# Dilated attention heads: the scaling of probabilities moves from VectorE to ScalarE

## The reference, cut to what matters

```python
DIL_GROUPS = ((128, 1), (512, 4), (2048, 16))

def dilated_window_group(q, k, v, window, dil):
    ...
    m = jnp.max(s, axis=-1, keepdims=True)
    p = jnp.exp(s - m)
    l = jnp.sum(p, axis=-1, keepdims=True)
    o = jnp.einsum('bnrhij,bnjrhe->bnirhe', (p / l).astype(v.dtype), vn)
    lse = (m + jnp.log(l))[..., 0]
    ...

def dilated_mixer(qkv):
    ...
    wts = jax.nn.softmax(jnp.stack(lses, 0), axis=0)
    o = jnp.sum(wts[..., None] * jnp.stack(outs, 0).astype(F32), axis=0)
```

## Time and profile before

| what | value |
|---|---|
| median of 3 runs | 2038.49 us (2036.68 to 2043.69) |
| the profiled execution | 2036.65 us, its span 2035.0 us |
| busy PE, DVE, ACT, POOL in the span | 1995.8, 1090.4, 822.8, 420.6 us |
| busy PE, DVE, ACT, POOL from 430 to 1045 us | 611.62, 332.21, 259.44, 188.87 us |
| granted PE clock | 0.997 as a mean |

### The profile page before, as it was taken

How to read it: one execution, slowest core, us unless ns; L and a number is a source line. 1 busy time by engine, 2 the same in 40 slices (tenths; PEclk the granted TensorE clock), 3 DMA queues, 4 the chain that set the end, 5 groups by cost and what they waited for, 6 DMA issues and landing times. The chain is left out here.

```text
span 2035.0 us, 27389 instructions
## 1 busy us (share of the span) xinstructions
PE 1995.8 (98%) x9949; PEld 1644.6 (81%) x9949; DVE 1090.4 (54%) x1952; ACT 822.8 (40%) x1496; POOL 420.6 (21%) x344
## 2 busy tenths in 40 slices
PE   7999999999999999999999999999999999999998
PEld 4688888888888888888888788788888888897787
DVE  7744444445545645645545532597878784335312
ACT  5433323343443433434524421555454533345322
POOL 2332413323323323323310011400101020000011
PEclk8999999999999999999999999999999999999999
DMA  7331331533332332332335421411111111341422
GB/s 250 121 132 64 123 124 42 150 94 81 76 104 62 95 104 61 95 103 62 95 125 173 135 72 35 141 32 35 50 31 52 31 52 42 125 121 61 155 62 104
DMA packets 218344, 186.84 MB, mean 92 GB/s; under 512 B 9498, under 2 KB 191236, under 8 KB 217604
## 3 DMA queue, kind: packets, MB, share of 16 engines
q1 hardware_dynamic: 212960, 177.56, 28.9%
q0 software_dynamic: 4480, 6.66, 1.4%
q10 hardware_dynamic: 804, 1.33, 0.2%
HBM read 144.27 MB, written 41.25 MB: 91 GB/s over the span
## 5 line engine op out<-in xcount | busy, mean ns | idle before, releaser
L298 DVE TENSOR_TENSOR w_lo<-w_raw,w_hi 128x512 fp32r<-128x512 f32 x219 | 195.1, 891 | 167.9 <-ACT w_hi L294 167.6
L218 PE MATMUL z_ps<-b_parts,w_hi 128*128 128x512 f32 x672 | 271.8, 404 | 2.3 <-ACT g_gate L228 1.8
L220 PE MATMUL z_ps<-b_parts,w_lo 128*128 128x512 f32 x672 | 265.2, 395 | 0.0
L219 PE MATMUL z_ps<-b_parts,w_hi 128*128 128x512 f32 x672 | 265.0, 394 | 0.0
L321 PE MATMUL z_ps<-ah_hi,w_hi 128*128 128x512 f32 x512 | 209.9, 410 | 5.0 <-DVE qkv L910 2.7
L323 PE MATMUL z_ps<-ah_hi,w_lo 128*128 128x512 f32 x512 | 202.1, 395 | 0.0
L322 PE MATMUL z_ps<-ah_lo,w_hi 128*128 128x512 f32 x512 | 201.9, 394 | 0.0
L294 ACT ACTIVATE w_hi<-w_raw 128x512 fp32r<-128x512 f32 x224 | 138.3, 624 | 104.1 <-PE z_ps L323 53.9
L200 DVE TENSOR_TENSOR w_lo<-w_raw,w_hi 128x1024 fp32r<-128x1024 f32 (+1 forms) x56 | 82.1, 1466 | 153.3 <-ACT w_hi L196 153.3
L218 PEld LDWEIGHTS z_ps<-b_parts,w_hi 128*128 128x128 f32 x672 | 126.7, 188 | 34.6 <-issue 7.1
L220 PEld LDWEIGHTS z_ps<-b_parts,w_lo 128*128 128x128 f32 x672 | 126.5, 188 | 29.7
(11 more groups left out here) (522 smaller groups left out, 4483.3 us busy)
## 6 DMA issues: line engine op xcount, KB each, us to landing
w_raw<-in_a_win SPq DMA_DIRECT2D x160, 256.0 KB, 3.3
w_raw<-in_b_win SPq DMA_DIRECT2D x33, 512.0 KB, 4.1
work<-in_a_win SPq DMA_DIRECT2D x48, 256.0 KB, 5.2
v_scratch<-qkv SPq DMA_DIRECT2D x12, 1024.0 KB, 5.2
work<-v_scratch SPq DMA_DIRECT2D x16, 512.0 KB, 5.4
y_scratch<-y SPq DMA_DIRECT2D x16, 512.0 KB, 3.3
w_raw<-in_a_wout SPq DMA_DIRECT2D x8, 768.0 KB, 5.6
w_raw<-in_b_wout SPq DMA_DIRECT2D x8, 768.0 KB, 6.0
```

Source lines behind the costliest of these rows:

```text
L218: pe.matmul(out, w_hi[slot][:, k, :], hi[k][:, tok], start=(k == 0), stop=False)
L219: pe.matmul(out, w_hi[slot][:, k, :], lo[k][:, tok], start=False, stop=False)
L220: mm = pe.matmul(out, w_lo[slot][:, k, :], hi[k][:, tok], start=False, stop=(k == nk - 1))
L298: eng.tensor_tensor(op_ring(w_lo, u), op_raw[i], op_ring(w_hi, u).bitcast(F32), ALU.subtract).then_inc(lo_op, 1)
```

## The change

ScalarE does all scaling of the probabilities. `scale_residues` (new, ACT) waits for `fac_done` and multiplies the four residue tiles with Copy activations whose scale is a column of factors; it stands right behind `weights`, in slots 27 and 31. `scale_natural` moves from DVE to ACT, behind `move_probs` in slots 30 and 34. DVE keeps the small steps of the join up to `fac`. The two kinds of tiles get semaphores of their own (`p_ready`, `p_natural`), and the turns wait for the one that is theirs. The computation is the same.

```diff
-                        pe.wait_ge(p_ready, 4 * h + which + 1)
+                        pe.wait_ge(p_natural if kind else p_ready, NS * h + which // 2 + 1)
...
+                    def scale_residues(h, s):
+                        act.wait_ge(fac_done, ordinal(h, s) + 1)
+                        for r in range(RES):
+                            out = act.activation(x[s][:, TPS + r, :], x[s][:, TPS + r, :], ACT.Copy, scale=fac[s][:, 1, r:r + 1])
+                        out.then_inc(p_ready, 1)
+
+                    def scale_natural(h, s):
+                        act.wait_ge(fac_in, 16 * ordinal(h, s) + 16)
+                        for t in range(TPS):
+                            out = act.activation(x[s][:, t, :], x[s][:, t, :], ACT.Copy, scale=fac_nat[s][:, t:t + 1])
+                        out.then_inc(p_natural, 1)
...
                         if u in (27, 31):
                             weights(h, 1 if u == 27 else 0)
+                            scale_residues(h, 1 if u == 27 else 0)
+                        if u in (30, 34):
+                            scale_natural(h, 1 if u == 30 else 0)
...
-                        dve.wait_ge(fac_done, n + 1)
-                        for r in range(RES):
-                            out = dve.tensor_scalar(x[s][:, TPS + r, :], x[s][:, TPS + r, :], fac[s][:, 1, r:r + 1], None,
-                                                    ALU.mult)
-                        out.then_inc(p_ready, 1)
-
-                    def scale_natural(h, s):
-                        dve.wait_ge(fac_in, 16 * ordinal(h, s) + 16)
-                        for t in range(TPS):
-                            out = dve.tensor_scalar(x[s][:, t, :], x[s][:, t, :], fac_nat[s][:, t:t + 1], None, ALU.mult)
-                        out.then_inc(p_ready, 1)
...
-                        if u in (30, 34):
-                            scale_natural(h, 1 if u == 30 else 0)
```

More of the change, by code:

```diff
@@ L938, in dilated @@
                  v_in, pv_done, gate_done, gate_out, gate_in, y_done, stat_out, stat_in, down_done, weight_done, join_step,
-                 fac_done, fac_out, fac_in, mem_in, v_out00, v_out01, v_out10, v_out11, *v_raw_in) = dil_sems = [nc.alloc_semaphore("dil_" + n) for n in (
+                 fac_done, fac_out, fac_in, mem_in, p_natural, v_out00, v_out01, v_out10, v_out11, *v_raw_in) = dil_sems = [nc.alloc_semaphore("dil_" + n) for n in (
                      "bias_in", "bias_ready", "qk_done", "max_done", "neg_done", "exp_done", "p_ready",
                      "tr_done", "pt_ready", "v_in", "pv_done", "gate_done", "gate_out", "gate_in", "y_done", "stat_out", "stat_in",
-                     "down_done", "weight_done", "join_step", "fac_done", "fac_out", "fac_in", "mem_in",
+                     "down_done", "weight_done", "join_step", "fac_done", "fac_out", "fac_in", "mem_in", "p_natural",
                      "v_out00", "v_out01", "v_out10", "v_out11", "v_a22_in", "v_a21_in", "v_a11_in", "v_a12_in")]
```

## The result

The changed kernel takes 2056.59 us in the median of 12 runs (2051.23 to 2060.64). The kernel before, run 12 times on the same chip, takes 2041.09 (2035.39 to 2048.16). The ratio is 1.0082 with an interval of 1.0068 to 1.0096: 0.8% slower. The forecast was 2049.3, so the sign was right and the time lies inside the range of 2041 to 2057.5, but the size was not: 10.8 us had been worked out, and the two medians are 15.5 apart.

A forecast was written before the change was run, and what follows sets the result against it. PE was taken to bound the dilated stage (busy 611.62 of 615.00 us). Added waits of +13.5 less 2.7 saved gave +10.8 us, 2036.65 to 2047.4 for the profiled execution; median forecast 2049.3, 0.53% slower, range 2041 to 2057.5.

The forecast's parts named there:

- F + 2.88: Second join: F is the end of `fac` on DVE; turn 3 on PE was to start at F + 2.90.
- The additions' 2.7: Second join: PE's four waits for DVE's additions of products were to vanish, -2.7 us.
- The natural tiles cost nothing: Slots 30 and 34: ACT's natural-tile scalings were to fit in idle time or before an eviction that waits anyway, zero.
- turns 0 and 2 do not wait: Dilated stage on PE: sign in the changed profile that these two turns start without waiting.
- turn 4 waits for no tile: Second join: residue tiles ready at F + 1.72, turn 4 starting at about F + 6.1, so no second wait.
- the first step: "0 to 0.2 later": First join, slot 27: scalings covered before turn 0; the statistics chain behind ACT's exponentials comes 0 to 0.2 us later.
- 14.2: Second join: turn 3's waits for ACT's copy of turn 2, summed over eight heads; 0.7 existed before, so +13.5 us.
- slower still: Rival: scaling at 0.54 a tile, +4.5 us, and statistics 0.5 later, +4; together 2057.8 us, chance 0.07.
- the second step: the last head taken as the others: First join: cover was worked out from the fourth head; the last head got only a turn 3 wait of 1.93.
- the third step: the clock as all or nothing: Rival: PE's clock halves for a slot behind each turn 3 wait, +26 us, 2075, chance 0.02; the sum had none.
- The ceiling of a gain, 3.4: Dilated stage: all PE waits together, 3.4 us or 0.17% of the kernel, the most that easing any engine could give.
- The first rival, a quicker join through DVE's silence: Second join comes at least 1.1 us sooner through quicker POOL DMAs, no turn 3 waits: -3.4 us, 2035.1, chance 0.07.

The follow-up runs named there:

- run 12: Not a label but a count: the kernel before, without the change, was run 12 times on the same chip, median 2041.09 us.
- last kernel: Changed kernel, but first-join scalings in slot 28 behind the last exponentials and second-join ones in slot 32 behind the copy of turn 2: 2030.92 us, ratio 0.9960.
- the kernel with the longer wait: Changed kernel plus twelve unused one-column copies on ACT behind the second join's scalings: 2061.80 us, ratio 1.0110.
- the second join alone: Against the kernel before, only the second join's residue scalings (slot 31) moved to ACT; first join and natural tiles stay on DVE: 2048.07 us, ratio 1.0047.

## Why the prediction was right and wrong

**Right: the mechanism and its clockwork.** ACT's four scalings take 1.71, with a step of 0.40; turn 3 starts at F + 2.88 (forecast 2.90). The additions' 2.7 is gone. The natural tiles cost nothing, turns 0 and 2 do not wait, turn 4 waits for no tile. ACT waits 15.3 / 16 = 0.96 for `fac` (forecast about 0.9).

The Trainium skill, ScalarE: Activation LUTs, rules for kernel authors, advises VectorE for multiplications. For the single tile the trace agrees: 344 ns undisturbed on VectorE against a step of 0.40 us on ScalarE. For the kernel that did not decide: with all 128 on ScalarE it is 0.4% faster when they stand behind the copy and the exponentials, and 0.8% slower when they stand ahead of them.

**Wrong, the first step: "0 to 0.2 later" for the second join.** I let the first join's scalings end under cover, since turn 0 wants them 4.1 later, and followed the exponentials behind them only by their sum. First join of the fourth head in the changed kernel, against the earlier trace rows:

```profile
698.28 0.17 DVE L1510 TENSOR_TENSOR fac<-down,inv 128x8 f32<-128x8 f32 x1
698.48 1.71 ACT L1347 ACTIVATE work<-work,fac 128x256 f32<-128x256 f32 x4 [0.94 <-DVE fac L1510]
700.10 0.63 ACT L901 ACTIVATE qkv<-z_ps 128x64 f32<-128x64 f32 x2
...
701.64 0.50 ACT L1337 ACTIVATE work<-work,both 128x256 f32<-128x256 f32 x1
...
702.54 0.76 POOL L1191 DMA_DIRECT2D stat_mem<-nat  x1 [0.25 <-ACT work L1337]
```

From the end of `fac` (698.45) to the issue of the statistics it is 4.09, where it was 696.61 - 692.71 = 3.90 before: that much was forecast. What came of it was more. In this head the second `fac` follows the first 14.96 later instead of 13.69. Three legs make it up: from the first `fac` to the issue of the statistics, from there to the issue of their return, and from there to `top` on DVE (the rest is DVE's own steps). By the timelines, in us:

```
                         to issue   to return   to top   steps   in all
fourth head, before        3.90        4.76      3.51     1.52    13.69
fourth head, after         4.09        5.52      3.72     1.63    14.96
mean of 8 heads, before    4.25        5.13      3.29     1.78    14.45
mean of 8 heads, after     4.64        5.30      3.61     1.64    15.18
mean of 8, last kernel     4.08        4.71      3.17     2.06    14.03
```

In heads 1, 4, 5 and 7 the issue comes 0.19 to 0.31 later and the first landing takes 0.25 to 0.84 longer. Of the 0.4 that the mean issue is late, 0.3 is the last head's. Seven heads came later, six of them by 0.5 to 1.3 and the last by 2.6; the third came 1.56 earlier. So the waits came to 17.8 in place of 14.2: the term was too small by 3.6 in this execution. That size is not settled: in the kernel with the longer wait, 22.8 less eight times 1.11 leaves 13.9. What is settled is the direction: with the first join's scalings on ACT ahead of the exponentials (five kernels) the second `fac` follows 14.70 to 15.18 later, with them on DVE or behind the exponentials (the five others) 13.95 to 14.45. Why the statistics land later when they are issued 0.2 later was not separated. The prediction had a rival for this, "slower still", with 0.07: 0.5 later, +4.

**Wrong, the second step: the last head taken as the others.** Its first join in the changed kernel:

```profile
1013.30 1.71 ACT L1347 ACTIVATE work<-work,fac 128x256 f32<-128x256 f32 x4 [0.84 <-DVE fac L1510]
...
1015.02 1.28 ACT L901 ACT_TABLE_LOAD   x1
...
1017.97 1.28 ACT L1335 ACT_TABLE_LOAD   x1
...
1020.26 0.57 ACT L901 ACTIVATE qkv<-z_ps 128x512 f32<-128x512 f32 x1
1020.66 0.77 POOL L1191 DMA_DIRECT2D stat_mem<-nat  x1 [3.04 <-ACT work L1337]
...
1020.89 0.50 PE L321 MATMUL z_ps<-ah_hi,w_hi 128*128 128x512 f32 x1 [1.11 <-ACT qkv L901]
```

The same join before:

```profile
997.70 0.17 DVE L1495 TENSOR_TENSOR fac<-down,inv 128x8 f32<-128x8 f32 x1
...
1002.32 0.57 ACT L901 ACTIVATE qkv<-z_ps 128x512 f32<-128x512 f32 x1
1002.72 0.77 POOL L1191 DMA_DIRECT2D stat_mem<-nat  x1 [1.03 <-ACT work L1337]
```

In this head, before and after, ACT changes its function twice between the first join and the last exponentials, 1.28 each time. There is no slack left: ACT's wait for `fac` and the scalings, 0.84 + 1.71 = 2.55, pass in full to the statistics (7.40 behind `fac` instead of 4.85). The eviction that follows the last exponentials is as late (1020.26, 7.00 behind `fac` instead of 4.45), and PE waits 1.1 for it. I had read the fourth head's first join and let it stand for all eight. All five kernels with the first join's scalings ahead of the exponentials have this wait of 1.1; none of the others has it.

**Wrong, the third step: the clock as all or nothing.** The rival had a fall behind every wait, +26, and 0.02. It came behind three of eight, 4.7 us, where the sum had nothing; the prediction named a fall as a sign of its being wrong. The row it was judged by, 2.4 of idle time without a fall, is a true row, but one row: waits of that length here were followed by a fall half of the time (below). The Trainium skill, TensorE: Matmul & The Clock Gate, HAM oscillation, warns that idle gaps of PE in a running kernel bring the clock down and up again; the runs agree, with 1.55 us for each fall.

Together: 3.6 + 1.1 + 4.7 = 9.4 on top of the 10.8, which makes 20.2 of the 20.5 in the profiled stage. The ceiling of a gain, 3.4, was a little low as well: the stage with no wait at all on PE is 5.0 shorter than before (600.63), and the 1.6 beyond the waits has no row.

**The first rival, a quicker join through DVE's silence, did not happen.** It rested on POOL's small DMAs landing sooner. One line's instructions in the changed kernel, L1191 and then L1195, against the earlier trace rows:

```profile
DMA to landing us min/median/max: 3.7/4.3/5.5
...
DMA to landing us min/median/max: 1.8/2.8/4.8
```

The medians were 4.2 and 2.4 before; neither fell. The Trainium skill, SBUF — State Buffer, who interferes with whom, by which VectorE's multiplications keep GpSimd from writing its descriptors, would have had them fall, and the changed kernel doesn't show it. In the last kernel, where DVE scales nothing either, the first is 3.6, and the second join comes 0.4 sooner than before (14.03 against 14.45). That does not tie it to DVE's silence: with 32 scalings on DVE the first is 3.9 and the step 13.95. The rival needed 1.1.

## What to carry to other kernels

Before an operation is moved to an engine with time to spare, read what stands behind it in that engine's list and who waits for it; the wait for its input (1.06 in the fourth head) and its own duration (1.71) hold all of that. Put the moved work behind the copy or the exponential that another engine wants and ahead of its own deadline, here one slot later. Work the sum out for the odd stage (the first and the last head) too, and allow for a wait of PE that costs more than its length, as nine of the fourteen waits over 2.05 us did here.

## What was not expected of the hardware

Single waits of PE in full work can cost more than themselves. Over the changed kernel, the second join alone and the longer wait, 24 waits of turn 3 can be compared. The ten of 2.05 us and less were followed by no slot at half clock. Of the ten from 2.07 to 2.84 five were, five were not, with no order by length (2.07 and 2.12 fell, 2.84 did not). The four from 2.94 to 3.75 all were. Each fall cost 1.55, within 0.1.

What was slow on DVE stood beside POOL's sums. The residue scalings of the kernel before, all 64 in one line (shortest, median, longest in ns), and those of the third head's second join with POOL's sum:

```profile
L1499 DVE TENSOR_SCALAR work<-work,fac x64: 334/352/1981, 460.5 to 1014.9; 128x256 f32<-128x256 f32 x64
```

```profile
630.45 2.76 DVE L1499 TENSOR_SCALAR work<-work,fac 128x256 f32<-128x256 f32 x4
631.48 1.30 POOL L281 TENSOR_TENSOR w_raw<-w_raw 128x512 f32<-128x512 f32 x1
```

The mean of 556 ns is not that of a typical one: 56 of the 64 take 0.33 to 0.40 us, and eight, the third of the four in each second join, 1.96 to 1.98. Each of the eight starts 0.50 to 0.52 before POOL's sum L281 and ends 0.16 behind its end. In the two other kernels that keep the second join on DVE the same one is as long; in the two that have only the first join there, none takes more than 0.41. In front of the additions that PE waited for, this is 1.6 us a head.

The low part of the weights shows the same. One line's group on DVE, 430 to 1060 us, for the changed kernel, the one before, and the second join alone (mean ns is the number behind the busy time):

```profile
L298 DVE TENSOR_TENSOR w_lo<-w_raw,w_hi 128x512 fp32r<-128x512 f32 x168 | 138.1, 822 | 161.9 <-ACT w_hi L294 161.9
```

```profile
L298 DVE TENSOR_TENSOR w_lo<-w_raw,w_hi 128x512 fp32r<-128x512 f32 x173 | 152.5, 882 | 114.2 <-ACT w_hi L294 113.9
```

```profile
L298 DVE TENSOR_TENSOR w_lo<-w_raw,w_hi 128x512 fp32r<-128x512 f32 x168 | 137.3, 817 | 146.4 <-ACT w_hi L294 146.2
```

The mean went from 882 to 822 ns at the same shape, but it is 817 in the kernel that keeps 96 of the 128 scalings on DVE: the scalings as such do not lengthen it. Before, 103 of the 166 low parts of the stage ran while POOL made no sum, and none of them took over 695 ns; the 63 that ran beside a sum took 1222 in the mean, up to 2151. The three kernels with the second join's scalings on DVE have means of 882 to 907, the seven others 817 to 857. No run moved the sums, so that they are the cause is read from the times and not tested. On ACT the scalings take 0.43 each (1.71 / 4) in either place. No matmul waited for a low part in this stage, before or after.
